# Stick-breaking attention in two rounded passes, and the modulation's row sums moved into the projections

## The reference, cut to what matters

```
# first block, 8 heads of 64, t = 16 + 512 positions
z = einsum('bqhd,bkhd->bhqk', q, k) * 0.125
strict = pos[k] < pos[q]
log_keep = where(strict, log_sigmoid(-z), 0)
later = cumsum(log_keep, axis=k, reverse=True) - log_keep
a = where(strict, exp(log_sigmoid(z) + later), 0)
y = einsum('bhqk,bkhd->bqhd', a, v)
# second block
mod = silu(c) @ w_ada + b_ada          # [1,1024] @ [1024,6144]
```

## Time and profile before

| | |
|---|---|
| median of three runs | 2781.6 us |
| the profiled execution, time / span | 2779.04 us / 2777.2 us |
| PE busy, whole span | 2492.1 us (90%) |
| DVE busy, whole span | 1613.9 us (58%) |
| projections, 21.60 to 204.82 | 183.2 us, PE busy 180.8, DVE busy 68.2 |
| attention, 204.82 to 318.35 | 113.5 us, PE busy 106.9, DVE busy 79.1 |

### The profile page before, as it was taken

How to read it: one execution, slowest core, us unless ns; L and a number is a source line. 1 busy time by engine, 2 the same in 40 slices (tenths; PEclk the granted TensorE clock), 3 DMA queues, 4 the chain that set the end, 5 groups by cost and what they waited for, 6 DMA issues and landing times.

```text
span 2777.2 us, 35683 instructions
## 1 busy us (share of the span) xinstructions
PE 2492.1 (90%) x14398; PEld 1975.2 (71%) x14398; DVE 1613.9 (58%) x3307; ACT 859.1 (31%) x1493; POOL 873.8 (31%) x787
## 2 busy tenths in 40 slices
PE   8999998898887787879899967799999999999999
PEld 7676565676444444468674556799999888888888
DVE  5247567552100000054536999899999876777775
ACT  3125333332000000033422248633333333333332
POOL 0003322001000100010001259655555565656662
PEclk9999999999999999969899978899999999999999
DMA  6635211235999999842004106799999999999995
GB/s 228 246 112 235 91 46 46 94 152 211 418 423 421 421 423 421 338 156 92 31 34 189 36 20 232 272 385 353 358 347 341 368 363 362 387 372 390 381 387 197
DMA packets 155097, 720.59 MB, mean 259 GB/s; under 512 B 15464, under 2 KB 30736, under 8 KB 125744
## 3 DMA queue, kind: packets, MB, share of 16 engines
q1 hardware_dynamic: 92096, 492.25, 45.0%
q0 software_dynamic: 62832, 226.00, 21.2%
HBM read 660.64 MB, written 57.16 MB: 258 GB/s over the span
## 4 chain that ended last, share of the span: by engine, by line
PE 52%; DVE 26%; DMA 13%; ACT 4%; issue 3%; POOL 2%; SPq 0%; POOLq 0%; DVEq 0%; ACTq 0%
DMA arena<-w 8%; PE psum L3383 7%; PE psum L1656 5%; DVE rounded L3462 5%; DVE arena L3513 5%; PE psum L442 4%; PE psum L2721 4%; PE psum L2186 4%; DMA arena<-v_rows,arena 3%; PE psum L971 3%; PE psum L3372 3%; PE psum L1663 2%; DVE arena L3498 2%; PE psum L3320 2%; POOL arena L3309 2%
## 5 line engine op out<-in xcount | busy, mean ns | idle before, releaser
L3383 PEld LDWEIGHTS psum<-rounded,rounded 128*128 128x128 f32 x3072 | 456.5, 190 | 30.4 <-issue 14.2
L3383 PE MATMUL psum<-rounded,rounded 128*128 128x320 f32 x3072 | 468.3, 313 | 11.0 <-DVE arena L3506 7.0
L3372 PEld LDWEIGHTS psum<-rounded,rounded 128*128 128x128 f32 x2880 | 425.1, 189 | 15.6 <-issue 6.7
L3372 PE MATMUL psum<-rounded,rounded 128*128 128x320 f32 x2880 | 431.4, 311 | 0.4 <-DVE rounded L3462 0.4
L3309 POOL DMA_INDIRECT arena<-u_rows,arena x192 | 288.9, 1505 | 243.6 <-DVE arena L3513 139.6
L1656 PE MATMUL psum<-arena 128*64 128x256 f32 x2048 | 257.6, 415 | 79.9 <-issue 53.0
L3401 ACT ACTIVATE rounded<-arena 128x1024 fp32r<-128x1024 f32 x248 | 255.8, 1049 | 226.8 <-PE psum L3383 162.3
L3309 POOL DMA_INDIRECT arena<-v_rows,arena x192 | 257.3, 1340 | 167.1 <-DVE arena L3524 55.6
L3462 DVE TENSOR_TENSOR rounded<-arena,rounded 128x1024 fp32r<-128x1024 f32 x248 | 302.6, 1220 | 7.0 <-ACT rounded L3401 5.4
L1656 PEld LDWEIGHTS psum<-arena 128*64 128x64 f32 x2048 | 182.9, 150 | 166.2 <-issue 115.1
L1779 DVE COPY arena<-psum 128x256 f32<-128x256 f32 x32 | 13.6, 425 | 441.3 <-PE psum L1706 441.3
(11 more groups left out here) (460 smaller groups left out, 3651.1 us busy)
## 6 DMA issues: line engine op xcount, KB each, us to landing
arena<-w SPq DMA_DIRECT2D x96, 2048.0 KB, 28.9
arena<-v SPq DMA_DIRECT2D x64, 1024.0 KB
arena<-uT SPq DMA_DIRECT2D x60, 1024.0 KB
arena<-wada SPq DMA_DIRECT2D x12, 2048.0 KB
arena<-wp SPq DMA_DIRECT2D x10, 2048.0 KB
arena<-gd SPq DMA_DIRECT2D x30, 640.0 KB
xb<-arena SPq DMA_DIRECT2D x1, 12032.0 KB, 48.8
gd<-arena SPq DMA_DIRECT2D x11, 1024.0 KB, 11.7
```

The costliest lines, as they stand in the source:

```text
L3372: ins = pe.matmul(PS[:, b, 0:DT], w[:, x, k, :], hv[:, y, :], k == 0 and i == 0, k == 7 and i == 2)
L3383: ins = pe.matmul(PS[:, b, 0:DT], w[:, y, x, :], gg[:, z, :], x == 0 and i == 0, x == 7 and i == 2)
```

## The change

1. `TRI`, `NEG` and the `sel` matrices are copied once to fp32r by POOL. Every masked `PT` tile is split by DVE in two instructions (`parts_dv`: a cast to fp32r, and the rest as a subtraction, also fp32r), behind POOL's mask. TRI, NEG and sel then each run as two fp32r matmuls, `hi` and `lo`, instead of one float32 matmul.
2. Ten of the twelve pieces of the modulation are computed during the projections. They come as 80 DMAs of 256 KB (one row of 512 each) into two sum buffers and four row buffers, in turn with the weights on SP's queue; 80 DVE steps stand after the chunks by the table `MOD_STEPS`, and the ten groups of columns stand on PE after chunks by `MOD_AT` and after value blocks. Bank 7 is kept for them, so the other banks are dealt out anew. Two pieces, 10 and 11, stay in the attention, one step after most tiles; their columns stand behind the last head.
3. POOL clears the block of zeros at the start of the attention, and the 16 MB of zeros are written to DRAM then, not in the projections; ACT waits for them after its last head. The first gate weights are fetched at the start of the attention, the second after the last sel.
4. In the attention ACT makes the softplus of the last tile after all four exponentials, and POOL masks keep 0, keep 1, a 2, keep 2, a 3, a 1, a 0, keep 3 instead of keep 0, a 2, a 3, a 1, keep 1, a 0, keep 2, keep 3.

```diff
+    MOD_AT = {5: 0, 7: 1, 8: 6, 10: 7, 12: 8, 15: 9}
+    MOD_STEPS = {1: 2, 2: 2, 3: 2, 4: 4, 5: 4, 6: 4, 7: 4, 8: 4, 9: 4, 10: 4, 11: 4, 12: 4, 13: 4}
...
+        def mod_pieces(a, b):
+            for n in range(a, b):
+                c, k = n // 8, n % 8
+                src = A["wada"][c][:, 512 * k:512 * k + 512]
+                if k == 0:
+                    if c > 1:
+                        sp.wait_ge(*P.pe["mod", c - 2])
+                    sp.dma_start(out=MOD_SUM[c % 2], in_=src).then_inc(*d_mod_sum[c % 2]("piece", c))
+                else:
+                    x = 7 * c + k - 1
+                    if x > 3:
+                        sp.wait_ge(*P.dv["mod", (x - 4) // 7, (x - 4) % 7 + 1])
+                    sp.dma_start(out=MOD_ROW[x % 4], in_=src).then_inc(*d_mod_row[x % 4]("piece", x))
...
+        def mod_columns(c):
+            pe.wait_ge(*P.dv["mod", c, 7])
+            for k in range(4):
+                ins = pe.matmul(PS[:, 7, 4 * c + k:4 * c + k + 1], MOD_SUM[c % 2][:, 128 * k:128 * k + 128], ONE[:, 0:1], True, True)
...
             ins.then_inc(*P.pe("chunk", j))
+            if j in MOD_AT:
+                mod_columns(MOD_AT[j])
...
+            if j:
+                mod_columns(1 + j)
         pe.wait_ge(*P.dv["ur"])
...
         for j in (1, 3):
             dv.wait_ge(*P.pe["va", j])
+            dv.tensor_copy(VA[:, j, :], PS[:, VA_BANK[j], :]).then_inc(*P.dv("va", j))
+            mod_steps(16 if j == 1 else 6)
...
             for kt in (3, 2, 1, 0):
-                pe.wait_ge(*S.po["keep", h, kt])
-                ins = pe.matmul(region(h, kt, 128 * kt), TRI, PT[i][kt], False, kt == 3)
+                pe.wait_ge(*S.dv["lower", h, kt])
+                for x in range(2):
+                    ins = pe.matmul(region(h, kt, 128 * kt), TRIR, halves_of[x][kt], False, kt == 3 and x == 1)
...
+    def parts_dv(dv, h, kt):
+        dv.wait_ge(*S.po["keep", h, kt])
+        dv.tensor_copy(PTH[h % 2][kt], PT[h % 2][kt]).then_inc(*S.dv("upper", h, kt))
+        dv.wait_ge(*S.dv["upper", h, kt])
+        dv.tensor_tensor(PTL[h % 2][kt], PT[h % 2][kt], PTH[h % 2][kt].bitcast(F32), ALU.subtract).then_inc(*S.dv("lower", h, kt))
...
-        for i in range(2):
-            sp.wait_ge(*S.pe["ada", 9 - i])
-            fetch(sp, i, i * RING, A["wp1"][6 + i], "gates", i)
+        sp.wait_ge(*S.pe["sel", 7])
+        fetch(sp, 1, RING, A["wp1"][7], "gates", 1)
```

More of the change, by code:

```diff
@@ L257, in build @@
     MT = at3(OW + 3 * TK, 8, META)
+    EARLY = 10
+    MOD_SUM = [at(o_qi + 512 * i, 512) for i in range(2)]
+    MOD_ROW = [at(x, 512) for x in (o_qi + 1024, o_qi + 1536, OW, OW + 5 * TK)]
     COS = at(OW + TK, TK)
@@ L293, in zeros_sp @@
     def zeros_sp(sp):
-        sp.wait_ge(*N1.dv["zero"])
+        sp.wait_ge(*S.po["zeros"])
         n0 = NX * CAP * 2 // 128
@@ L371, in norm1_po @@
         po.wait_ge(*d_in.end())
+        po.tensor_copy(TRIR, TRI).then_inc(*N1.po())
+        po.tensor_copy(NEGR, NEG).then_inc(*N1.po())
+        po.tensor_copy(SELR, CST[:, C_SEL:C_SEL + 240]).then_inc(*N1.po("constants"))
     P = Stage(counter, "proj", "pe ac dv")
@@ L603, in proj_dv, with mod_steps @@
         RX = RN[:, META:TK]
+        done = [0]
+        def mod_steps(count):
+            for _ in range(min(count, 8 * EARLY - done[0])):
+                c, k = done[0] // 8, done[0] % 8
+                done[0] += 1
+                total = MOD_SUM[c % 2]
+                if k == 0:
+                    dv.wait_ge(*d_mod_sum[c % 2]["piece", c])
+                    dv.tensor_scalar(total, total, SC8[:, 0:1], None, ALU.mult).then_inc(*P.dv("mod", c, 0))
+                else:
+                    x = 7 * c + k - 1
+                    dv.wait_ge(*d_mod_row[x % 4]["piece", x])
+                    dv.wait_ge(*P.dv["mod", c, k - 1])
+                    dv.scalar_tensor_tensor(total, MOD_ROW[x % 4], SC8[:, k:k + 1], total, ALU.mult, ALU.add).then_inc(
+                        *P.dv("mod", c, k))
+        dv.wait_ge(*N1.ac["cond"])
         ahead(0)
@@ L701, in build @@
     EM = EX[1][0]
+    PTH = [[alias(RING + 1280 * i + OFF[kt], NQ[kt])[:, :] for kt in range(4)] for i in range(2)]
+    PTL = [[alias(OW + 2560 * i + 1280 + OFF[kt], NQ[kt])[:, :] for kt in range(4)] for i in range(2)]
     AFTER = {3: (), 2: (2,), 1: (3, 1), 0: (0,)}
@@ L776, in scores @@
             scores_of(pe, h)
+        pe.wait_ge(*N1.po["constants"])
         for h in range(8):
@@ L811, in stick_pe @@
                 bank[6] = S.dv["ya", j]
+        claim(5)
+        for c in (10, 11):
+            pe.wait_ge(*S.dv["ada", c, 7])
+            for k in range(4):
+                ins = pe.matmul(PS[:, 5, 4 * (c - 10) + k:4 * (c - 10) + k + 1], late_sum(c)[:, 0, 128 * k:128 * k + 128],
+                                ONE[:, 0:1], True, True)
+        ins.then_inc(*S.pe("ada"))
         pe.wait_ge(*S.ac["meta a"])
@@ L904, in stick_po @@
     def stick_po(po):
+        po.wait_ge(*P.pe["chunk", 20])
+        po.memset(ZERO, 0.0).then_inc(*S.po("zeros"))
         for h in range(8):
-            for made, x in (("keep", 0), ("a", 2), ("a", 3), ("a", 1), ("keep", 1), ("a", 0), ("keep", 2), ("keep", 3)):
+            for made, x in (("keep", 0), ("keep", 1), ("a", 2), ("keep", 2), ("a", 3), ("a", 1), ("a", 0), ("keep", 3)):
                 if made == "a":
```

156 lines of the change are left out of this document (83 added, 73 removed).

## The result

The changed kernel takes 2794.7 us as the median of 16 runs (2787.3 to 2802.4), the kernel before 2778.9 in the same rounds (16 runs, 2766.9 to 2788.5): ratio 1.0057, 95% interval 1.0042 to 1.0072. It is slower, by 15.8 us. The profiled execution took 2800.3 us, its span is 2798.4.

What follows compares the result with a forecast made beforehand. TensorE was taken to bound the projections, ScalarE and GpSimd the changed attention's heads. 2779.0 + 36 (projections) - 17 (attention) = 2798, or 2800 as a median; range 2783 to 2820.

Steps and rivals of the forecast that it cites:

- Columns: Projections: ten pieces of eight column matmuls each, 0.96 us a piece, add 9.6 us on the full TensorE.
- The step that comes too late: Projections: TensorE waits for VectorE's steps behind chunks 8, 10 and 12, 3.9 us each, 11.7 us; piece 9 adds 1.3.
- UR: Projections: vm waits for UR behind 22 VectorE steps and row loads, 6.8 us instead of 1.4, so 5.4 more.
- The clock in the projections: Projections: four new stalls each bring a dip of TensorE's clock, 2 us each, 8 us, bounds 0 and 13.
- The attention: Attention: 88.6 us against 113.5 at the full clock, 24.9 less; dips ahead of y cost 8: -17 us.
- The clock that stays up: Rival: no clock dips in either stage, 28.0 - 24.9 = +3 us, 2785; chance 0.13.
- The third: Rival: slow clock in every head and after every stall for the longest time seen, +32 us, 2814; chance 0.25.
- The first: Rival: y follows sel without a wait, heads take TensorE's 8.9 us, attention 42.8 less, median 2774; chance 0.07.

Runs made afterwards that it cites:

- e11: The changed kernel itself measured again, beside the kernel with filled waits: median 2798.6 us, ratio 1.0083 to the kernel before.
- e9: e2 plus e6's and e7's moves, kr rotation earlier, last eight early steps as two fours, weights of chunks 17 to 20 fetched earlier: 2745.9 us, ratio 0.9877.
- e1: Changed kernel with the columns of pieces 6, 7, 8 and 9 one chunk later: 2779.2 us, ratio 1.0033 to the kernel before.
- e2: e1 with VectorE's copy of UR moved ahead of the eight steps before the values: 2768.8 us, ratio 0.9983 to the kernel before.
- e10: e4's kernel measured again, beside the changed kernel: 2789.0 us, ratio 1.0048 to the kernel before.
- e6: e2 with the attention's sixteen late steps moved to the heads' ends: 2761.5 us, ratio 0.9943 to the kernel before.
- e3: Changed kernel without the ten early pieces of the modulation (no loads, steps or columns): 2755.6 us, ratio 0.9941 to the kernel before.
- e7: e2 with exponentials a3, a1, a0 ahead of the next head's tile 2 softplus, their masks ahead of keep 2: 2755.4 us, ratio 0.9917.
- e4: Changed kernel with useless matmuls filling TensorE's waits ahead of the columns of pieces 6 to 9 and vm: 2791.4 us, ratio 1.0076.

## Why the prediction was right, and where its numbers were off

The forecast was 2800 as a median and slower; it is 2794.7 and slower. The profiled execution came out at 2800.3 where the sum had 2798, but that closeness is luck: against the sum the projections cost 8.7 us more than the 36 forecast, the attention gave 3.3 more than the 17, and the unchanged rest and the start happened to be 3.2 shorter. The median lies 5.6 below this execution, where I had put it 2 above. The two stages alone give +24.4, where 36 - 17 had been +19, and the second measurement of the same kernel (e11) has +24.4 in its median.

**Columns.** Forecast 9.6 for ten pieces. Measured 9.7 at the full clock (80 records in e9).

**The step that comes too late.** Forecast 3.9 us behind chunks 8, 10 and 12, and this came as told, released by VectorE's step. The chain has 125.33 to 129.27, 144.22 to 148.16 and 163.64 to 167.57: 3.9 each. Piece 9 was put at 1.3, between 0 and 3; of 14.0 us of waits the other three leave 2.2. e1 shows the cause: with the columns one chunk later, these waits are 0.6 us.

**UR.** Forecast a wait of 6.8 in place of 1.4; measured 7.8. The mechanism was right, steps of piece 5 and 6 wait for rows. The term that was short is the row's way: 3.1 us from issue to use, from a write; the three rows that led to UR took 4.17 to 4.51 (2.65 to 5.97 in e11, whose wait is 9.5). e2 takes the wait away by moving one copy.

**The clock in the projections: the term that was too small.** Forecast "2 us each, 8 us, with bounds 0 and 13". What the waits and the columns leave of 44.7 is 44.7 - 9.7 - 11.9 - 2.2 - 6.4 = 14.5, above the upper bound. In e11, the same kernel, it is 44.3 - 9.7 - 14.4 - 8.1 = 12.1, within it. Filling the waits gave back 10.8 (e10 against e11); e1's busy time of PE fell by 9.8 with the records unchanged. There were five dips where four were forecast, piece 9's short wait had one too, and each was longer than taken: 0.50 for 5.0 to 6.8 us of work at the columns and vm (3.1 to 6.8 in e11), which is 2.5 to 3.4 us each. I had read the length of a dip off one at 218 that lasted 3.4 us, and kept the longer one at 266 as a bound only. The projections of the kernel before hold one of 6.8 us themselves (163.6 to 170.4), which I had not read; at half the clock it is 3.4 us. Filling costs something itself, and some waits stay partly open in e10 (1.4 at the columns, 1.0 at vm), so 10.8 is a lower figure.

**The attention.** Forecast heads of 10.5 to 11.5, 11.0 without steps and 11.8 with, and 8 us for the clock. Measured at the full clock: 10.5 without steps (all heads of e6), 11.8 with steps (head 2 of e3). PE's busy time in the stage is 77.2 us, and 70.7 for the same 361 records in e6, where the clock is 1.00 throughout: the clock took 6.6. So the wait ahead of y for GpSimd, behind ScalarE's softplus of tile 2, was right, and was shown by e7, which takes the order away and gets 9.5 to 10.0. The dips came behind y's wait in the four heads with a step, not in seven with 1.1 us each. Of the 3.3 us that the stage is shorter than forecast, 1.4 are the clock (6.6 for 8) and 1.9 the heads at the full clock (86.7 for 88.6). The last head is 8.4 us, as forecast, and TRI, NEG and sel in two passes take 4.2 (336.16 to 340.35).

**The rivals.** The clock that stays up (2785) is refuted by the stretches at 0.50. The third (2814), a dip in every head, is refuted by heads 0 and 1, though in the projections the dips were as long as it said. The first (2774), heads of 8.9, did not come, though it is the interesting one: heads of 9.5 do exist (e7, e9), once the masks of the weights no longer stand behind keep 2.

## What to carry to other kernels

A step put on an idle engine is free only if it is ready before the busy engine asks for it: count, for each consumer, how many steps are queued ahead of it, and place the consumer one whole unit of work later than the arithmetic says. Here one table entry per piece, one copy moved up, eight steps spread and one fetch of weights moved ahead turned +44.7 us into +9.3. In an order that is written by hand, look at what stands in front of the result that the busy engine wants, on every engine of the path: one softplus, one sum and one mask of the next head cost 1 us a head in GpSimd's queue and a step on VectorE another 1.4. And judge by stages: from L878 on all these kernels run the same code, and single profiled executions took 2447.0 (e4) to 2472.5 us (e9) for it, more than most of the effects in question.

## What the runs showed of the hardware

- Three waits of TensorE of 3.9 us in the changed kernel were followed by 5.0 to 6.8 us at 1.2 GHz (3.4 to 6.8 in e11), and so cost another 1.7 to 3.4 us of matmul time each. A wait of 1.6 us ahead of y in e6 brought no fall in any of seven heads. Longer ones went both ways in heads of the same code: 2.44 (e11, head 3) and 2.60 (changed, head 3) brought one, 2.60 (e2, head 3) and 2.97 (e3, head 2) did not.
- The clock also falls with TensorE busy without a break, in 64 matmuls of 8 columns: 6.8 us at 0.50 in the kernel before, 13.7 in e2.
- Useless matmuls in a wait gave back matmul time: 96 of them in five waits, 9.0 (e4) and 10.8 us (e10) less in the stage. The medians are 9.6 apart in one pair of measurements and show no gain in the other.
- 256 KB rows that stream behind one another on SP's queue landed 4.2 to 4.5 us after issue where UR hung on them (2.7 to 6.0 in e11), while the median of those in the projections is 3.3 and a 256 KB write took 2.6.
- One VectorE step of 0.78 us ahead of a mask made TensorE's wait 1.4 us longer, not 0.8: the four masks ahead of y took 0.7 us longer (2.18 instead of 1.48), between the two lengths of the earlier trace rows.
